# Block 1's first feed-forward products by Strassen's algorithm, with the sums of the weights made in DRAM

## What is computed

```python
h = rms_norm(x, g_mlp[l])
x = x + jnp.square(jax.nn.relu(h @ w_ff1[l])) @ w_ff2[l]     # w_ff1: 1024 x 4096, w_ff2: 4096 x 1024
```

## Time and profile before

| | |
|---|---|
| runs of the kernel before | 1617.12 us median of 3 (1614.49 to 1618.69) |
| the profiled execution | 1608.34 us, span 1606.5 us |
| TensorE, VectorE, ScalarE, GpSimd busy in the span | 1534.5, 821.0, 617.6, 355.4 us |
| f1 and f2 stage with its two first tiles, 482 to 832 us | 350 us, TensorE busy 349.61 |
| attention of block 1, merge, w_out | to 300, to 433, to 482 us |

### The profile page before, as it was taken

One profiled execution on the slowest core, in us unless ns is written; L12 is line 12 of the kernel. 1 busy time (PEld: TensorE's weight loads), 2 busy tenths in 40 slices (PEclk: granted clock), 3 DMA queues, 4 the chain that ended last, 5 costly groups with the idle time before them and its releaser, 6 DMA issues.

```text
span 1606.5 us, 19519 instructions
## 1 busy us (share of the span) xinstructions
PE 1534.5 (96%) x7198; PEld 1219.5 (76%) x7202; DVE 821.0 (51%) x1644; ACT 617.6 (38%) x1118; POOL 355.4 (22%) x364
## 2 busy tenths in 40 slices
PE   6899989999999999999999999989999999999995
PEld 5687655688877888888888788856687888888884
DVE  6537566444444343343446697577364543443444
ACT  5423467422244222232346333556443322222222
POOL 3200345300020000000036524445441210220112
PEclk9999999999999999999999999999999999999998
DMA  5743300332233233323332653311422232332321
GB/s 193 131 108 95 103 1 14 112 98 93 91 92 92 92 92 96 101 92 104 93 98 68 155 148 119 112 47 56 155 90 81 92 105 93 95 102 92 101 79 56
DMA packets 46669, 154.11 MB, mean 96 GB/s; under 512 B 5698, under 2 KB 5890, under 8 KB 46576
## 3 DMA queue, kind: packets, MB, share of 16 engines
q1 hardware_dynamic: 41840, 137.63, 27.0%
q0 software_dynamic: 4736, 15.25, 4.6%
HBM read 142.78 MB, written 9.55 MB: 95 GB/s over the span
## 4 chain that ended last, share of the span: by engine, by line
PE 85%; DVE 8%; ACT 3%; issue 2%; DMA 1%; DVEq 0%; POOL 0%; SPq 0%; another core or an unknown queue 0%; ACTq 0%
PE PSA L578 83%; PE PSA L780 1%; DVE WL L1691 1%; DVE AR L1781 1%; ACT AR L1298 1%; DVE AR L1779 1%; PE PSA L924 1%; DMA WR<-w_in 1%; DVE AR L1806 0%; DVE AHL L1897 0%; ACT AHL L1346 0%; ACT WH L1226 0%; DVE AR L2274 0%; DVE AR L2367 0%; DMA AR<-AR 0%
## 5 line engine op out<-in xcount | busy, mean ns | idle before, releaser
L578 PE MATMUL PSA<-Ah,WH 128*128 128x512 f32 x1072 | 425.6, 397 | 18.7 <-DVE WL L1691 18.3
L578 PE MATMUL PSA<-Ah,WL 128*128 128x512 f32 x1072 | 420.7, 392 | 0.0
L578 PE MATMUL PSA<-Al,WH 128*128 128x512 f32 x1072 | 420.6, 392 | 0.0
L1226 ACT CAST WH<-WR 128x1024 fp32r<-128x1024 f32 (+3 forms) x234 | 240.8, 1031 | 227.7 <-PE PSA L578 222.6
L1691 DVE TENSOR_TENSOR WL<-WR,WH 128x1024 fp32r<-128x1024 f32 (+3 forms) x207 | 251.5, 1216 | 73.1 <-ACT WH L1226 72.6
L578 PEld LDWEIGHTS PSA<-Ah,WH 128*128 128x128 f32 x1072 | 203.5, 190 | 65.1 <-issue 22.3
L578 PEld LDWEIGHTS PSA<-Al,WH 128*128 128x128 f32 x1072 | 203.4, 190 | 42.9 <-issue 0.7
L578 PE MATMUL PSA<-Bh,WH 128*128 128x512 f32 (+1 forms) x592 | 230.6, 390 | 5.4 <-DVE Bl L1968 4.0
L578 PEld LDWEIGHTS PSA<-Ah,WL 128*128 128x128 f32 x1072 | 203.1, 189 | 42.8
L578 PE MATMUL PSA<-Bh,WL 128*128 128x512 f32 (+1 forms) x592 | 229.2, 387 | 0.0
L578 PE MATMUL PSA<-Bl,WH 128*128 128x512 f32 (+1 forms) x584 | 226.7, 388 | 0.0
(11 more groups left out here) (363 smaller groups left out, 1934.7 us busy)
## 6 DMA issues: line engine op xcount, KB each, us to landing
WR<-w_in SPq DMA_DIRECT2D x228, 512.0 KB, 3.5
gt_tmp<-AR SPq DMA_DIRECT2D x16, 256.0 KB, 2.2
WR<-w_in SPq DMA_DIRECT2D x8, 384.0 KB, 3.1
XT<-scr_tmp POOLq DMA_DIRECT2D x8, 264.0 KB, 12.1
XT<-xT_in SPq DMA_DIRECT2D x4, 512.0 KB, 8.2
XT<-scr_tmp POOLq DMA_DIRECT2D x8, 256.0 KB, 15.9
XT<-xT_in POOLq DMA_DIRECT2D x1, 2048.0 KB, 9.9
x_tmp<-XT POOLq DMA_DIRECT2D x1, 2048.0 KB, 7.6
```

The lines of the kernel that those rows point to most:

```text
L578: return pe.matmul(o, l, r, start=start, stop=stop)
L1226: ac.copy(WH[p][:, 0:n], WR[j % RAW][:, 0:n]).then_inc(w_hi, 1)
```

## The change

Four f1 tiles stay as they were, in front of q = 0. The other 28 output chunks are taken in 14 pairs (two in q = 0, four in each other q). For a pair, the product of its 256 outputs by 1024 inputs with 1024 inputs by 512 tokens is cut in 2 x 2 quarters: the two output chunks, inputs 0 to 511 and 512 to 1023, tokens 0 to 255 and 256 to 511. Strassen's algorithm in Winograd's form makes 7 products of quarters in place of 8. Each is 4 chunks x 3 matmuls of 256 columns (`product`).

- The sums of the activations' quarters are made once: ScalarE copies x times the gain into GX while w_out's products run, VectorE makes four sums for each of four chunk pairs (TS), ScalarE and VectorE split them (TSH, TSL).
- The four sums of the weights' quarters are made in DRAM, in `ws`, by eight transfers on GpSimd's queue for each group of pairs, four of them adding ones; the first group ahead of `add_squares("m1")`, the three others behind it.
- A pair has four weight tiles t1: three of 1024 columns (half from `w`, half from `ws`, so two transfers each) and one of 512.
- The 7 products go to banks 2 to 5. ScalarE copies one of them, VectorE adds them up with two double and three single sums of quarters, rectifies, and ScalarE and VectorE square and split as before, the second chunk of a pair first.
- Two more pairs of buffers WH, WL are used by the t1 tiles (`place`: the one unused for longest; other tiles keep the three in turn), and splits are made when their buffer comes free, up to five tiles ahead (`due`, `due_beside`). The first f2 tile waits for two chunks at a time.

With the code's rule the order of the splits in pairs 1, 5, 9 and 13, ahead of f2, is: pair 1 splits the first f2 tile at `due(j)` and the next two at `due(j + 3)`; the three others split the first f2 tile at `due(j + 1)`, the next two at `due(j + 2)` and none at `due(j)` and `due(j + 3)`. Pair 0 splits t1 2 to 5 at `due(j)`; t1 0 and 1 are split before it.

```diff
-        t += [("f1", 8 * q + i, 1024, True) for i in range(8)]
+        t += [("f1", i, 1024, True) for i in range(4 if q == 0 else 0)]
+        t += [("t1", 4 * p + r, 1024 if r < 3 else 512, True) for p in range(*PAIRS1[q]) for r in range(4)]
...
+        loads[j % RAW] += 32 if name == "t1" and n == 1024 else 16
+        ld_at[j] = loads[j % RAW]
         if split:
+            p = min(range(SPL + 2), key=lambda p: last_use[p]) if name == "t1" else n_hi_ % SPL
+            place[j], free_at[n_hi_], last_use[p] = p, last_use[p], n_mm_
...
+        WHP = [*WH, ARR[:, 8192:9216], ARR[:, 13696:14720]]
+        WLP = [*WL, ARR[:, 9216:10240], ARR[:, 14720:15744]]
...
+        def free_stop(done, stop):
+            return next((u for u in range(stop) if free_at[u] > done), stop)
+        def due(j):
+            return free_stop(mm_no[j], stop_of[j] + 5)
+        def due_beside(i):
+            j = tid["f2", i]
+            return free_stop(mm_no[j] - 1, stop_of[j] + (5 if i < 24 else 2))
...
+                if name == "t1":
+                    p, r = i // 4, i % 4
+                    summed, c = next(ws_sum[q] for q in range(4) if p < PAIRS1[q][1])
+                    sp.wait_ge(summed, c + 128)
+                    if r < 3:
+                        own = slice(0, 512) if r == 0 else slice(512, 1024)
+                        sp.dma_start(W[:, own], d["w"][j, :, own]).then_inc(s, 16)
+                    c = 512 if r == 0 else 0
+                    sp.dma_start(W[:, c:c + 512], d["ws"][p, r, :, :]).then_inc(s, 16)
...
+            def product(ws, c, b, c0, src):
+                for k in range(4):
+                    last = chunk((ws[0][:, c:c + 512], ws[1][:, c:c + 512]), src, k, bank(b)[:, c0:c0 + 256], 4)
+                return last
...
+            def pair1(p):
+                j = tid["t1", 4 * p]
+                if p == 0:
+                    pe.wait_ge(f_re, 4)
+                    pe.wait_ge(f_dv.sem, f_dv.end("l"))
+                else:
+                    pe.wait_ge(f_dv.sem, f_dv.at("c", 5 * (p - 1) + 1))
+                ws = halves_ready(j)
+                product(ws, 0, 2, 0, quarter(0, 0))
+                product(ws, 512, 2, 256, sums_of(2)).then_inc(w_mm, 1)
+                ws = halves_ready(j + 1)
+                product(ws, 0, 3, 256, sums_of(1))
+                product(ws, 512, 3, 0, quarter(4, 0)).then_inc(w_mm, 1)
+                if p:
+                    pe.wait_ge(f_dv.sem, f_dv.at("c", 5 * (p - 1) + 3))
+                ws = halves_ready(j + 2)
+                product(ws, 0, 4, 256, sums_of(0))
+                product(ws, 512, 4, 0, sums_of(3)).then_inc(w_mm, 1)
+                if p:
+                    pe.wait_ge(f_dv.sem, f_dv.at("c", 5 * (p - 1) + 4))
+                ws = halves_ready(j + 3)
+                product(ws, 0, 5, 0, quarter(4, 256)).then_inc(w_mm, 1)
...
+                if q == 0:
+                    feat2(tid["f1", 0], hA, [bank(2), bank(3)], wait_norm("m1"), lambda: sums("m1"))
+                    for n in range(2, 4):
+                        feat(tid["f1", n], hA, 8, bank(2 + n))
+                for p in range(*PAIRS1[q]):
+                    pair1(p)
...
+                    pe.wait_ge(f_hi, 8 * q + k - k % 2 + 2)
+                    pe.wait_ge(f_lo, 8 * q + k - k % 2 + 2)
...
+            def squares1(n):
+                ac.activation(Bh[:, n % 8, :], RF[n % 4], ACT.Square).then_inc(f_hi, 1)
+                ac.activation(RF[n % 4], RF[n % 4], ACT.Square).then_inc(f_ac.sem, 1)
...
+                    if ph == 1:
+                        ac.activation(GX[i], x3[:, i, 0:T], ACT.Copy, scale=gain[:, i:i + 1]).then_inc(f_ac.sem, 1)
                     square(nm, i)
+                    if ph == 1 and i > 4:
+                        sums_high(i - 5)
+                if ph == 1:
+                    sums_high(3)
                 log_table()
+            def sums_high(k):
+                ac.wait_ge(f_dv.sem, f_dv.at("x", 3 * k + 2))
+                ac.copy(TSH[k], TS[k]).then_inc(f_ac.sem, 1)
...
+                    j, n = tid["t1", 4 * p], 2 * p + 4
+                    result(j)
+                    if p > 1:
+                        ac.wait_ge(f_dv.sem, f_dv.at("c", 5 * (p - 2)))
+                    ac.copy(CU[p % 2][0], bank(2)[:, 0:256]).then_inc(f_ac.sem, 1)
+                    split_units(due(j))
+                    result(j + 1)
+                    split_units(due(j + 1))
                     ac.wait_ge(f_re, n + 1)
-                    if n > 3:
-                        ac.wait_ge(f_lo, n - 3)
-                    ac.activation(RT[s + 1], RT[s], ACT.Square).then_inc(f_sq, 1)
-                    if q and i == 0:
-                        result(tid["f2", 8 * q - 1])
-                    ac.activation(Bh[:, i, :], RT[s], ACT.Square).then_inc(f_hi, 1)
-                    if n == 7:
+                    if q and n % 8 == 0:
+                        result(tid["f2", n - 1])
+                    squares1(n + 1)
+                    split_units(due(j + 2))
+                    ac.wait_ge(f_re, n + 2)
+                    squares1(n)
+                    split_units(due(j + 3))
...
+                t1, t2, t3, t4 = (TS[k][:, 256 * t:256 * t + 256] for t in range(4))
+                dv.wait_ge(f_ac.sem, f_ac.at("g0", i) if i < 6 else f_ac.at(f"g{i}"))
+                if i < 4:
+                    dv.tensor_tensor(t1, GX[k][:, 256:512], GX[k][:, 0:256], ALU.subtract).then_inc(f_dv.sem, 1)
+                    return
+                dv.wait_ge(f_dv.sem, f_dv.at("d", k))
+                dv.tensor_tensor(t2, t1, GX[4 + k][:, 256:512], ALU.subtract).then_inc(f_dv.sem, 1)
+                dv.tensor_tensor(t3, GX[4 + k][:, 256:512], GX[k][:, 256:512], ALU.subtract).then_inc(f_dv.sem, 1)
+                dv.wait_ge(f_dv.sem, f_dv.at("x", 3 * k))
+                dv.tensor_tensor(t4, GX[4 + k][:, 0:256], t2, ALU.add).then_inc(f_dv.sem, 1)
...
+            split_to(tid["f1", 1])
+            for k in range(4):
+                sums_low(k)
...
+                rectified(bank(2 + n), RF[n])
+                if n < 1:
+                    split_to(tid["f1", 3])
+                if n > 1:
+                    split_to(tid["f1", n] + 2)
+                squares_low(n, f_ac.at("s", n))
...
+                    (c1, u2, u3, u4), first, second = CU[p % 2], RF[n % 4], RF[n % 4 + 1]
+                    def added(m):
+                        dv.wait_ge(f_dv.sem, f_dv.at("c", 5 * p + m))
+                    result(j + 1)
+                    dv.wait_ge(f_ac.sem, f_ac.at("c", 3 * p))
+                    dv.tensor_tensor(RU[p % 2], halves(bank(3)), twice(c1), ALU.add).then_inc(f_dv.sem, 1)
+                    added(0)
+                    dv.tensor_tensor(u3, bank(2)[:, 256:512], u2, ALU.add).then_inc(f_dv.sem, 1)
+                    split_units(due(j))
+                    result(j + 2)
+                    added(1)
+                    dv.tensor_tensor(halves(second), halves(bank(4)), twice(u3), ALU.subtract).then_inc(f_dv.sem, 1)
+                    dv.tensor_tensor(u4, bank(4)[:, 256:512], u2, ALU.subtract).then_inc(f_dv.sem, 1)
+                    added(2)
+                    rectified(second, second)
+                    split_units(due(j + 1))
+                    result(j + 3)
+                    added(3)
+                    dv.tensor_tensor(first[:, 256:512], bank(5)[:, 0:256], u4, ALU.subtract).then_inc(f_dv.sem, 1)
+                    added(4)
+                    rectified(first, first)
+                    squares_low(n + 1, f_ac.at("c", 3 * p + 1))
+                    split_units(due(j + 2))
+                    squares_low(n, f_ac.at("c", 3 * p + 2))
+                    split_units(due(j + 3))
...
+            def sums_of_weights(q):
+                (p0, p1), (d_ws, c) = PAIRS1[q], ws_sum[q]
+                j0, j1 = tid["t1", 4 * p0], tid["t1", 4 * p1 - 4] + 1
+                a11, a21, a12, a22 = (d["w"][j0 + o:j1 + o:4, :, c0:c0 + 512] for o, c0 in ((0, 0), (0, 512), (1, 512), (2, 512)))
+                s3, s2, s1, s4 = (d["ws"][p0:p1, r, :, :] for r in range(4))
+                pl.dma_start(s1, a21).then_inc(d_ws, 16)
+                pl.dma_start(s3, a21).then_inc(d_ws, 16)
+                pl.wait_ge(d_ws, c + 32)
+                pl.dma_start(s1, a22, accum_op=ALU.add).then_inc(d_ws, 16)
+                pl.dma_start(s3, a11, accum_op=ALU.add).then_inc(d_ws, 16)
+                pl.wait_ge(d_ws, c + 64)
+                pl.dma_start(s2, s1).then_inc(d_ws, 16)
+                pl.wait_ge(d_ws, c + 80)
+                pl.dma_start(s2, a11, accum_op=ALU.add).then_inc(d_ws, 16)
+                pl.wait_ge(d_ws, c + 96)
+                pl.dma_start(s4, s2).then_inc(d_ws, 16)
+                pl.wait_ge(d_ws, c + 112)
+                pl.dma_start(s4, a12, accum_op=ALU.add).then_inc(d_ws, 16)
...
+            sums_of_weights(0)
             add_squares("m1")
+            for q in range(1, 4):
+                sums_of_weights(q)
...
```

(60 more changed lines are left out.)

103 lines of the change are left out of this document (54 added, 49 removed).

## The result

The changed kernel takes 1759.94 us (median of 4 executions, 1757.60 to 1763.52), the kernel before 1615.80 beside it: a ratio of 1.0899, with an interval of 1.0862 to 1.0936. The profiled execution took 1763.52 us, its span is 1761.7. I had forecast 1617.5 us, 1611.5 to 1625.5. The kernel is 144 us slower, and nothing in the range allowed for it.

A forecast was written before the change was run, and what follows sets the result against it. TensorE was taken to bound the kernel, busy 328.00 of 328.00 us in the changed stretch. Terms: -11.2 + 1.15 + 2.7 + 7.5 + 0.3 = +0.4 us, giving 1617.5 us on the median, range 1611.5 to 1625.5.

The forecast's parts named there:

- each of the three groups is 8 MB, half of it added, 40 to 60 us at 210 GB/s: On GpSimd's queue, each later group of weight sums in DRAM takes 40 to 60 us, hidden with at least 25 us to spare.
- "0.3" us for the transfers: Loads of a pair beside the sums in DRAM: 0 to 3 us of cost, taken as 0.3.
- Between one and two copies: Price of a DRAM transfer that adds, which had no row: between one and two plain copies.
- Rival D: Sums in DRAM and doubled loads share the DMA engines, t1 tiles come late: slower, 1626 us; chance 0.16.
- The gain: TensorE in the 14 pairs: 256-column matmuls start 0.120 us apart, saving 0.80 us per pair, 11.2 us in all.
- Rival C: TensorE's 256-column matmuls start 0.109 us apart, load wholly hidden: gain 16.6 us, time 1612; chance 0.04.
- VectorE: Within pairs VectorE needs about 8.9 of 10.08 us, keeps up with TensorE and is 90 to 97% busy.
- Rival E: VectorE's sums from PSUM last 0.1 to 0.2 us longer and set a pair's pace, 10.5 us: 1624 us; chance 0.10.
- The waits: New TensorE waits: 1.15 us ahead of pair 0, 2.7 within it, 7.5 at three f2 boundaries; 11.3 in all (8.8 to 15.2).
- at each boundary: End of pairs 5, 9, 13: TensorE waits 2.2 us for f2 splits, up to 3.6 if VectorE lags; taken as 2.5.
- Rival B: Waits at the f2 boundaries and in pair 0 are half those derived, VectorE being early: 1611 us; chance 0.12.
- The margin of SyncE's load: Second group's adding ends before SyncE's load of t1 8, issued at 541 us; TensorE misses that load from about 564.

## Why the prediction was wrong, point by point

**The step that failed** is a term of the sum: "each of the three groups is 8 MB, half of it added, 40 to 60 us at 210 GB/s", and with it "0.3" us for the transfers. It measured 137 us per group and some 150 us on the stage. I took the bound from 2 MB between DRAM and SBUF, whose transfers have 128 partitions outermost, and moved it to transfers whose outermost dimension is 2 or 4, without asking over how many engines they go. "Between one and two copies" was a good bound for the adding (24.6 us against 13.6); the copy was mis-sized, by the engines. The range had no end for that case, though nothing in the trace of before excluded it.

**Rival D had the mechanism.** It named the place (SyncE's wait for the second group), the measure (a chain over 86 us) and the price past it, "a microsecond each". It gave 1626 with a chance of 0.16, since I priced it for a small excess only. Applied at each of the three waits, its rule gives 51 us for a chain of 137, three times: about 153, against 150.3 measured on the stage. The four-engine copies, 98 us, give 3 x 12 = 36 by it; measured 402.0 - 363.65 = 38.4. The rule was sound and its input wrong. A rival whose price grows by the microsecond belongs in the range as far as its input can go.

**The gain: right.** In the pairs the 256-column matmuls start 0.12 us apart; here after the last long wait:

```profile
911.24 0.40 PE L634 MATMUL PSA<-Ah,ARR 128*128 128x256 f32 x2
911.48 0.28 PE L634 MATMUL PSA<-Al,ARR 128*128 128x256 f32 x1
911.60 0.40 PE L634 MATMUL PSA<-Ah,ARR 128*128 128x256 f32 x2
911.84 0.28 PE L634 MATMUL PSA<-Al,ARR 128*128 128x256 f32 x1
```

Three in 0.36 us, a pair in 10.08 us. The run with the waits moved gives 10.0 us for 14 pairs, against 11.2, with 0.5 us of waiting and a few short steps still in it. Rival C (0.109 apart) is out.

**VectorE: right in its cost, wrong in its share.** A 256-wide sum lasts 0.42 us, and a dependent one starts 0.72 us behind a 512-wide one, as forecast. In the run without sums the 13 operations of a full pair stand back to back from 590.13 to 599.19 us, 9.1 us where I had 8.9, and TensorE waits for VectorE nowhere within a pair from the second on. Rival E is out. But over each run of four pairs (586.2 to 626.4 us and the two after it) VectorE is busy 75 to 77%, not the 90 to 97% that I named: it starts some 4 us into the run, and the last pair has fewer splits.

**The waits: right in kind, 1.6 us too dear.** In the run without sums, as lengthenings of TensorE's spacing: ahead of pair 0 0.95 us (forecast 1.15), at t1 2 2.63 (2.7), at each boundary 1.73 at the start and 0.31 more at chunk 6, 2.04 (2.2, taken as 2.5). The sum is 9.7 us (11.3). That VectorE would fall further behind over a run of four pairs, for which I had added 0.3 each, did not happen. Rival B (half the waits) is out.

**What I had no term for: the clock.** Behind the wait at t1 2 TensorE's granted clock falls. Windows of the run without sums (PE busy, its loads, DVE, ACT, POOL, clock, DMA share, GB/s):

```profile
524.00:527.00 3.00, 2.33 (x11) 2.36 (x12) 3.00 (x4) 0.00 (x0) 0.00 (x0) 0.61 0.39 137
527.00:530.00 3.00, 3.00 (x23) 3.00 (x23) 1.08 (x3) 1.05 (x1) 0.00 (x0) 0.82 0.95 293
530.00:533.00 3.00, 3.00 (x27) 3.00 (x27) 2.97 (x6) 1.66 (x3) 0.00 (x0) 1.00 0.44 182
```

The wait of 2.47 us ends at 524.67, and until about 528.2 the 256-column matmuls start 0.21 apart instead of 0.12, which is the lower of the two levels. It costs some 1.7 us. Gain 11.2, waits 9.7 and clock 1.7 make +0.2 of the +0.6 us measured. About the rest lies behind the six waits at the boundaries: the second matmul starts 0.31 us after the first there instead of 0.23, 0.5 us together. That the engines' part still came out near my sum (+0.6 for +0.1) is luck: the waits that I had overdone by 1.6 us happened to pay for the clock.

**The margin of SyncE's load.** I said that the adding would be over before 541 us and that it would be wrong "if SyncE stands at the load of t1 8". It stood there until 623.48, the sign that I had named myself.

## What to carry to other kernels

Before a new transfer is priced from an old one, compare their outermost dimensions: a transfer with 2 or 4 outermost leaves most of the 16 DMA engines idle, and putting the rows outermost, or several transfers in flight, gave back all but 0 to 6 of the 144 us here. Where a chain of transfers is hidden "with a margin", write down the rate at which the margin is gone, and let the range reach to the slowest rate that no row excludes. A change whose gain and new waits both come out as forecast can still be worth having once the waits are moved: this one is 0.3 to 0.5% faster than the kernel before with two small changes of order.

## What the runs showed of the hardware

- A copy of 1 MB within DRAM with an outermost dimension of four takes 12.4 to 16 us, an adding one 24.6 us with nothing beside it (48 GB/s written), with four packets of 2048 bytes in flight; with the rows outermost mostly 14 to 20 are in flight, and it takes 10.5 us beside loads. Half a MB with an outermost two has two in flight and takes about as long as 1 MB with four: medians of 26.2 and 24.4 us over all steps from the packed weights.
- Four transfers with an outermost four at once don't share four engines: 62 us per group, as fast as with 128 rows outermost (65 to 73).
- TensorE waits 2.5 us for t1 2 in all the runs that keep that wait, but its granted clock falls behind it in only four of the traces (the kernel after, rows outermost, no sums, one transfer per pair), to starts 0.21 apart for some 3.5 us. In the four others (early f2 splits, 4 x 32 blocks, copies on four and on 16 engines) it stays 1.00. So the same wait costs 1.7 us more in one execution than in another; what decides it is open. After 35 us of idle time, at 904 us in the kernel after, the starts are 0.21 apart until about 909.
- 28 MB of transfers within DRAM beside the weights' loads, with the DMA engines 79% busy from 486 to 700 us, cost TensorE nothing where nobody waited for them (a stage of 363.65 us with and without). With the changed kernel's larger loads, at 93%, one load came late enough to cost 1.6 us.
